# Which engine multiplies attention's probabilities, and which copies the turned ones

## The chip, the cores and the metric

One core of one Trainium2 chip runs the whole layer. The metric is the device time of one execution in microseconds (us); three runs of the kernel before are given. A change of about 0.2% can be told from none.

## The reference

One decoder layer over x of 4096 tokens by 1024 channels, float32. The normed input goes through one projection, whose columns feed three groups of heads of width 64: six heads A (sliding window of 128, two key heads, a learned sink), six heads B (dilated attention, three patterns of 1, 4 and 16 tokens' stride whose results are joined), four heads C (cross-attention to 256 memory tokens). Each result is gated, all go through one output projection, a norm and the residual. The part that the change touches, cut:

```python
p = jnp.exp(s - m[..., None])
denom = jnp.sum(p, axis=-1)
if sink is not None:
    denom = denom + jnp.exp(sink_b - m)
o = jnp.einsum('nbhgqk,nbkhd->nbqhgd', p, vw.astype(jnp.float32))
o = o / jnp.moveaxis(denom, -1, 2)[..., None]
...
wts = jax.nn.softmax(jnp.stack(lses, axis=0), axis=0)
ob = jnp.sum(wts[..., None] * jnp.stack(outs, axis=0), axis=0)
```

## The kernel before, in words

Three stages follow each other: the projection (`project_stage`), attention (`attend_stage`), and the output projection with the norm (`finish_stage`). Before 1053 us the trace is the first stage, after about 1840 us the last.

In attention, `head_group` is built three times, for B, then A, then C. A head is worked in two phases, one for each half of the 4096 queries. A phase has units, each of 128 queries against 256 keys (128 at the sequence's start), and the units go in pairs: 24 pairs a phase for B (12 phases), 8 for A (12 phases) and for C (8 phases), 448 pairs in all. A pair goes through these steps:

- `scores` on TensorE (lines 1353 and 1354): two matmuls a unit into PSUM `ps_s`, which has three places for B and four for A and C; `scores_ready`.
- `scores` on VectorE (line 1455): adds the mask, negates, takes the row maximum while it moves the scores from PSUM to `probs` in SBUF; `max_ready`.
- `scores` on ScalarE (line 1621): the exponential in place, with the row's sum; `sums_ready`.
- Once a phase is through, its coefficients are worked out: for A and C a reciprocal (lines 1471 and 1473), for B an exchange of some dozen small steps (lines 1489 to 1534) that weighs the three patterns; `coef_ready`.
- `scale` (line 1544): VectorE multiplies each unit's probabilities in place by a coefficient for each query; `weighted`.
- `turn` (line 1424): TensorE transposes the pair into PSUM `ps_t`, which has two places; `turned`.
- `copy` (line 1645, or 1648 and 1649 where the two units differ in size): ScalarE copies it to SBUF `pT`, which has four places; `turned_copied`.
- `times_values` (line 1408): TensorE multiplies it with the values, two pairs at a time after each odd pair's next turn; `values_done`. For B the far pattern's banks are kept by ScalarE (line 1658) and added by VectorE (line 1575); the bank is gated by VectorE (lines 1599 and 1609).

The order on each engine is written out by `rounds` and `slots_of`: in a round the new scores of phase a stand beside the turning and multiplying of the phase before, c, and the end of the one before that, b. The slots carry one pair each. Within a slot TensorE does `scores`, `turn`, `exchange`, then `times_values`; VectorE does the `scale` of the pair three slots ahead, `scores`, `copy_queries`, then the read-out of banks; ScalarE does `copy`, `keep`, `scores`, then `copy_queries`. For B the turning of a phase starts 18 slots after its round does, for A and C four; the coefficients come in slot 14 for B and slot 1 for A and C.

`copy_queries` puts B's queries into two further orders, 512 columns at a time: four instructions a phase on ScalarE (line 1674) and four on VectorE (line 1553). A's are shared between the two (lines 1662 and 1555). GpSimd's queue in attention holds seven DMAs that bring parts of the output weights (lines 1921 and 1927), each behind a wait for a finished phase of A or C. All other loads and stores are on SyncE's queue.

In the first stage GpSimd adds weight quarters (lines 943 to 954), casts the first queries (lines 996 and 1004), and VectorE subtracts the rounded part of the weights (line 570) and joins products (lines 621, 644, 739).

Of the kernel before, what the change touches and what calls it, by code (L numbers as in the profile page):

```python
# [27 lines left out]
P = 128  # L28
# [1065 lines left out]
def head_group(nc, io, sc, kind, buf, ctx, prev):  # L1094
# [56 lines left out]
    natural_copied = sem("natural_copied") if kind == "B" else None  # L1151
    k_loaded = [[sem(f"k_loaded{i}{s}") for s in range(2)] for i in range(2)]
    later_keys = buf.early.later_keys
# [5 lines left out]
    scores_ready, max_ready, sums_ready = sem("scores_ready"), sem("max_ready"), sem("sums_ready")  # L1159
    weighted, turned, turned_copied = sem("weighted"), sem("turned"), sem("turned_copied")  # L1160
    values_done = sem("values_done")
    bank_read = sem("bank_read")
    coef_ready = sem("coef_ready")
    step, exps_ready = sem("step"), sem("exps_ready")
    if kind == "B":
# [10 lines left out]
    def number(phase):  # L1176
        return phase[0] * 2 + phase[1]
# [4 lines left out]

    TOTAL = 2 * heads * NP

    def loads(sp):
# [123 lines left out]
    def tensor_parts(pe):  # L1309
# [65 lines left out]
        def times_values(phase, e):  # L1375
# [9 lines left out]
            if kind == "B" and e == 8:  # L1385
                pe.wait_ge(v_loaded[s], 32 * (h + 1))
            pe.wait_ge(turned_copied, p * NP + e + 1)
            bank = bank_of[2 * e]
# [25 lines left out]
        def turn(phase, e):  # L1414
            h, s = phase
            p = number(phase)
            pe.wait_ge(weighted, p * NP + e + 1)
            if prev and isinstance(p, int) and p == 0 and e < 2:
                pe.wait_ge(prev.turned_copied, prev.TOTAL + e - 1)
            ge(pe, turned_copied, p * NP + e - 1)  # L1420
            for j in range(2):
                u = FLAT[s][2 * e + j]
                for at in range(2 - len(u.tiles), 2):
                    last = nc.tensor.transpose(ps_t[:, e % 2, j, at * P:(at + 1) * P],  # L1424
                                               probs[:, s, 2 * e + j, at * P:(at + 1) * P], ident[:])
            last.then_inc(turned, 1)
        return named(scores=scores, exchange=exchange, turn=turn, times_values=times_values)

    def vector_parts(dve):
# [105 lines left out]

        def scale(phase, e):
            h, s = phase
            p = number(phase)
            if e == 0:
                dve.wait_ge(coef_ready, p + 1 + C1)  # L1540
            for j in range(2):
                u = FLAT[s][2 * e + j]
                place = probs[:, s, 2 * e + j, 2 * P - u.keys:]
                last = nc.vector.tensor_scalar(place, place, coef[:, s, u.column:u.column + 1], None, ALU.mult)  # L1544
            last.then_inc(weighted, 1)

        def copy_queries(phase, slot):
            p = number(phase)
            if kind == "B" and slot in N_SLOTS and p > 0:
                if N_SLOTS[slot] == 0:  # L1550
                    dve.wait_ge(q_loaded, 32 * p)
                    dve.wait_ge(scores_ready, p * NP)
                nc.vector.tensor_copy(*natural_piece(N_SLOTS[slot])).then_inc(natural_copied, 1)
            if kind == "A":
                copy_natural(dve, phase, slot, lambda p, g: nc.vector.tensor_copy(
                    *natural_part(p, 2 + g)).then_inc(q_copied, 1))
# [44 lines left out]
        def gated(phase, d):  # L1601
# [7 lines left out]
            nc.vector.tensor_tensor(by, summed.rearrange("p u (r a) -> p u r a", a=32), by, ALU.mult).then_inc(y_ready, 1)  # L1609
        return named(scores=scores, exchange=exchange if kind == "B" else inverse, scale=scale, finish=finish, finish_rest=finish_rest, gated=gated, copy_queries=copy_queries)  # L1610

    def scalar_parts(act):
# [23 lines left out]
        def copy(phase, e):  # L1636
            h, s = phase
            p = number(phase)
            act.wait_ge(turned, p * NP + e + 1)
            if prev and isinstance(p, int) and p == 0 and e < 4:  # L1640
                act.wait_ge(prev.values_done, prev.TOTAL + e - 3)
            ge(act, values_done, p * NP + e - 3)
            a = [2 * P - FLAT[s][2 * e + j].keys for j in range(2)]
            if a[0] == a[1]:
                nc.scalar.activation(pT[:, e % 4, :, a[0]:], ps_t[:, e % 2, :, a[0]:],  # L1645
                                     ACT.Copy).then_inc(turned_copied, 1)
            else:
                nc.scalar.activation(pT[:, e % 4, 0, a[0]:], ps_t[:, e % 2, 0, a[0]:], ACT.Copy)
                nc.scalar.activation(pT[:, e % 4, 1, a[1]:], ps_t[:, e % 2, 1, a[1]:],
                                     ACT.Copy).then_inc(turned_copied, 1)  # L1650

# [8 lines left out]
        def copy_queries(phase, slot):  # L1660
            if kind == "A":
                copy_natural(act, phase, slot, lambda p, g: nc.scalar.activation(
                    *natural_part(p, g), ACT.Copy).then_inc(q_copied, 1))
            p = number(phase)
            if kind != "B" or slot not in Q_SLOTS or isinstance(p, int) and p == 0:
                return
            i = Q_SLOTS[slot]
            if i == 0:
                act.wait_ge(scores_ready, p * NP)
                act.wait_ge(q_loaded, 32 * p)  # L1670
            by = by_residue(q[:, 0, :])
            to = q[:, 1, i * CHUNK:(i + 1) * CHUNK].rearrange("p (b i a) -> p b i a", i=4, a=8)
            of = by[:, 4 * i:4 * i + 4, :].rearrange("p i (b a) -> p b i a", a=8)
            nc.scalar.activation(to, of.bitcast(F32), ACT.Copy).then_inc(q_copied, 1)
        return named(scores=scores, exchange=exchange, copy=copy, keep=keep, copy_queries=copy_queries)

    return named(
        kind=kind, heads=heads, phases=2 * heads, NP=NP, NS=NS, TAIL=TAIL, EARLY=EARLY, TOTAL=TOTAL,
        scores_ready=scores_ready, values_done=values_done, max_ready=max_ready, turned=turned,
        turned_copied=turned_copied, bank_read=bank_read, coef_ready=coef_ready, done_sem=done_sem, y_stored=y_stored,  # L1680
        q_copied=q_copied, copied_by=copied_by, natural_copied=natural_copied,
        loads=loads, tensor_parts=tensor_parts, vector_parts=vector_parts, scalar_parts=scalar_parts)


# [8 lines left out]
def attend_stage(nc, io, sc, early, probs, ahead):  # L1693

    with ExitStack() as ctx:
# [58 lines left out]
        def vector_round(a, c, b):  # L1754
            for i, slot in enumerate(slots_of(a, c, b)):
                if c and c.g.kind != "B":
                    c.parts.exchange(c.phase, i)
                if slot.ahead:
                    x, e = slot.ahead
                    x.parts.scale(x.phase, e)  # L1760
                for v in slot.new:
                    a.parts.scores(a.phase, v)
                if a:
                    a.parts.copy_queries(a.phase, i)
# [12 lines left out]
        def scalar_round(a, c, b):  # L1777
            for i, slot in enumerate(slots_of(a, c, b)):
# [10 lines left out]
                if a:  # L1789
                    a.parts.copy_queries(a.phase, i)  # L1790

        def rounds(eng, round_, parts_of):
# [15 lines left out]
        with nc.Block() as block:  # L1808
# [105 lines left out]
            def _(pool):  # L1914
# [14 lines left out]

                for n in range(4):  # L1930
                    pool.wait_ge(A.done_sem, (9 + n) * NC)
                    load_sum(n)
                for n in range(3):
                    pool.wait_ge(C.done_sem, (1 + n) * NC)
                    load_w(n)
                for g in (B, A):
# [449 lines left out]
```

## Time and profile before

| what | value |
|---|---|
| median of 3 runs | 2163.92 us (2161.46 to 2164.92) |
| span of the profiled execution | 2163.3 us |
| TensorE matmul busy | 2054.7 us (95%) |
| TensorE weight load busy | 1717.7 us (79%) |
| VectorE busy | 1557.3 us (72%) |
| ScalarE busy | 1351.1 us (62%) |
| GpSimd busy | 114.9 us (5%) |
| mean granted TensorE clock | 0.973 |

The execution's own time, outside of its span, isn't given apart from the runs' times above. Busy shares are over the whole span, and the stages differ. PE stands for TensorE's matmuls, PEld for its weight loads, DVE for VectorE, ACT for ScalarE, POOL for GpSimd, SP for SyncE; L1544 is line 1544 of the kernel. A matmul's end is modelled. The granted clock is 1.00 at 2.4 GHz and 0.50 at 1.2 GHz. `a_` stands before the names of attention's own tiles.

### The profile page before, as it was taken

The numbers are of one execution on the slowest core, as the hardware profiler recorded it, in microseconds if no ns is written. First come the engines' busy times: TensorE is split into PE (matmuls) and PEld (weight loads), VectorE is DVE, ScalarE is ACT, GpSimd is POOL, SyncE is SP. The second block draws the span as 40 slices with busy tenths as digits, with TensorE's granted clock in tenths as the row PEclk, the third lists the DMA queues.
The fourth block names the chain that finished last, engine by engine and source line by source line (L and its number), as shares of the span: only waits on it lengthen the run. The fifth ranks groups of instructions, "written<-read, shape, count | busy, mean of one in ns | idle before, by whom it ended". The sixth has DMA issues, their size and how long they took to land. (4 is left out here: it accounts for less than half of the span.)

```text
span 2163.3 us, 39340 instructions
## 1 busy us (share of the span) xinstructions
PE 2054.7 (95%) x12892; PEld 1717.7 (79%) x12892; DVE 1557.3 (72%) x4410; ACT 1351.1 (62%) x3520; POOL 114.9 (5%) x116
## 2 busy tenths in 40 slices
PE   5999899999999999999899999999899998999998
PEld 4787678888888888888777887888778887788886
DVE  6564674546664574446588989989799997888887
ACT  6454454544555464343699979989689998533333
POOL 1232310000000000002000000000000000000000
PEclk7999999999999999999799989989999999999999
DMA  4477576777577657589778676686869996245543
GB/s 157 144 243 217 170 240 179 221 242 218 154 225 223 219 182 244 199 276 273 179 147 157 133 142 135 131 166 121 166 149 214 232 270 179 98 158 175 174 158 113
DMA packets 351737, 401.40 MB, mean 186 GB/s; under 512 B 105617, under 2 KB 255249, under 8 KB 346689
## 3 DMA queue, kind: packets, MB, share of 16 engines
q1 hardware_dynamic: 343120, 364.80, 61.5%
q0 software_dynamic: 8432, 34.30, 5.1%
q8 instruction: 97, 1.59, 0.3%
q14 instruction: 88, 0.71, 0.1%
HBM read 255.62 MB, written 143.39 MB: 184 GB/s over the span
## 5 line engine op out<-in xcount | busy, mean ns | idle before, releaser
L854 PE MATMUL p_ps<-p_u_hi,p_w_hi 128*128 128x512 f32 x1344 | 534.7, 398 | 25.8 <-DVE p_p_c L739 10.6
L856 PE MATMUL p_ps<-p_u_hi,p_w_lo 128*128 128x512 f32 x1344 | 526.8, 392 | 0.0
L855 PE MATMUL p_ps<-p_u_lo,p_w_hi 128*128 128x512 f32 x1344 | 526.2, 392 | 0.0
L570 DVE TENSOR_TENSOR p_w_lo<-p_w_raw,p_w_hi 128x512 fp32r<-128x512 f32 x336 | 245.7, 732 | 331.4 <-ACT p_w_hi L423 329.8
L1621 ACT ACTIVATE probs<-probs,a_stat 128x256 f32<-128x256 f32 (+1 forms) x896 | 433.7, 489 | 49.2 <-DVE a_stat L1455 45.8
L423 ACT ACTIVATE p_w_hi<-p_w_raw 128x512 fp32r<-128x512 f32 x336 | 210.7, 628 | 331.7 <-PE p_ps L856 303.7
L854 PEld LDWEIGHTS p_ps<-p_u_hi,p_w_hi 128*128 128x128 f32 x1344 | 254.1, 189 | 86.1 <-DVE p_u_lo L577 12.0
L856 PEld LDWEIGHTS p_ps<-p_u_hi,p_w_lo 128*128 128x128 f32 x1344 | 254.0, 189 | 54.5
L1455 DVE CUSTOM_DVE_ANT_0 probs<-a_ps_s,fixed 128x256 f32<-128x256 f32 (+1 forms) x704 | 251.6, 396 | 63.2 <-PE a_ps_s L1354 61.9
L855 PEld LDWEIGHTS p_ps<-p_u_lo,p_w_hi 128*128 128x128 f32 x1344 | 254.4, 189 | 50.7
L1408 PE MATMUL a_ps_o<-a_pT,a_v 128*64 128x128 f32 x3320 | 256.7, 285 | 22.8 <-ACT a_pT L1645 21.5
L1424 PE MATMUL a_ps_t<-fixed,probs 128*128 128x128 f32 x1660 | 260.3, 278 | 5.9 <-ACT a_pT L1645 5.1
L1544 DVE TENSOR_SCALAR probs<-probs,a_coef 128x256 f32<-128x256 f32 (+1 forms) x896 | 263.3, 338 | 3.0
L1408 PEld LDWEIGHTS a_ps_o<-a_pT,a_v 128*64 128x64 f32 x3320 | 181.9, 138 | 79.2 <-ACT a_pT L1645 43.8
L1645 ACT ACTIVATE a_pT<-a_ps_t 128x512 f32<-128x512 f32 (+1 forms) x412 | 229.4, 560 | 16.8 <-PE a_ps_t L1424 16.6
L1353 PE MATMUL a_ps_s<-k_hi,q 128*128 128x256 f32 (+1 forms) x672 | 217.3, 342 | 13.0 <-PEq L266 5.9
L1424 PEld LDWEIGHTS a_ps_t<-fixed,probs 128*128 128x128 f32 x1660 | 196.3, 143 | 12.4 <-DVE probs L1544 6.7
L1354 PE MATMUL a_ps_s<-k_lo,q 128*128 128x256 f32 (+1 forms) x672 | 191.7, 302 | 0.0
L1621 ACT ACTIVATION_READ_ACCUMULATOR probs<-probs,a_stat 128x1 f32 x896 | 175.4, 196 | 0.0
L1353 PEld LDWEIGHTS a_ps_s<-k_hi,q 128*128 128x128 f32 x672 | 136.8, 204 | 43.3 <-issue 31.0
L2228 PE MATMUL f_ps<-f_w_lo,parts_hi 128*128 128x512 f32 x384 | 150.4, 392 | 0.0
L2227 PE MATMUL f_ps<-f_w_hi,parts_hi 128*128 128x512 f32 x368 | 144.6, 393 | 5.2 <-DVE probs L2143 4.1
(202 smaller groups left out, 2756.5 us busy)
## 6 DMA issues: line engine op xcount, KB each, us to landing
p_w_raw<-in_w_in SPq DMA_DIRECT2D x156, 256.0 KB, 3.6
p_w_raw<-scratch_w_s SPq DMA_DIRECT2D x144, 256.0 KB, 3.7
scratch_qk_hi<-p_out_a SPq DMA_DIRECT2D x80, 256.0 KB, 4.1
scratch_qk_lo<-p_out_b SPq DMA_DIRECT2D x80, 256.0 KB, 4.2
a_v<-scratch_v SPq DMA_DIRECT2D x40, 512.0 KB, 7.6
scratch_gate<-p_out_a SPq DMA_DIRECT2D x64, 256.0 KB, 3.9
scratch_v<-p_out_a SPq DMA_DIRECT2D x256, 64.0 KB, 2.3
a_gate<-scratch_gate SPq DMA_DIRECT2D x64, 256.0 KB, 5.9
```

Of the source, the lines that this page charges most:

```text
L423: nc.scalar.activation(w_hi[:, m % 3, :, :], w_raw[:, entry(j, g), :, :], ACT.Copy).then_inc(w_hi_ready, 1)
L570: nc.vector.tensor_tensor(w_lo[:, m % 3, :, :], w_raw[:, entry(j, g), :, :], w_hi[:, m % 3, :, :].bitcast(F32), ALU.subtract).then_inc(w_l ...
L854: nc.tensor.matmul(bank, hi, u_hi[j][:, k, :], start=j < 2 and k == 0, stop=False, skip_group_check=True)
L855: nc.tensor.matmul(bank, hi, u_lo[j][:, k, :], start=False, stop=False, skip_group_check=True)
L856: last = nc.tensor.matmul(bank, lo, u_hi[j][:, k, :], start=False, stop=k == KH - 1, skip_group_check=True)
L1353: nc.tensor.matmul(out, w, keys_of(keys_hi, u), start=True, stop=False)
L1408: last = nc.tensor.matmul(place_of(ps_o[j * HD:(j + 1) * HD, bank % 2, :], u), v[name][:, half, tile, :], pT[:, e % 4, j, at * P:(at + 1) ...
L1424: last = nc.tensor.transpose(ps_t[:, e % 2, j, at * P:(at + 1) * P], probs[:, s, 2 * e + j, at * P:(at + 1) * P], ident[:])
L1455: last = nc.vector.tensor_tensor_reduce(out=probs[:, s, 2 * slot + j, a:], in0=ps_s[:, slot % NS, j, a:], in1=masks[u.kind][:, a:], scale= ...
L1544: last = nc.vector.tensor_scalar(place, place, coef[:, s, u.column:u.column + 1], None, ALU.mult)
L1621: last = nc.scalar.activation(place, place, ACT.Exp, scale=-1.0, bias=stat[:, s, 0, u.column:u.column + 1], accum_out=stat[:, s, 1, u.colu ...
L1645: nc.scalar.activation(pT[:, e % 4, :, a[0]:], ps_t[:, e % 2, :, a[0]:], ACT.Copy).then_inc(turned_copied, 1)
```

## The change

The 896 multiplications by coefficients go from VectorE to GpSimd, whose program in attention becomes a round of its own, with its seven DMAs put behind the last multiplication of certain phases. Of the turned pairs, each fourth (number 3, 7, 11, ... in its head group) is copied by VectorE, behind `scores` in its slot; ScalarE copies the others. B's queries that ScalarE put in order are put so by VectorE. The semaphore of the copies becomes two, one for each copying engine, and some semaphores that a head group doesn't use are no longer made. The diff, cut:

```diff
-    weighted, turned, turned_copied = sem("weighted"), sem("turned"), sem("turned_copied")
+    weighted, turned = sem("weighted"), sem("turned")
+    turned_copied = (sem("turned_copied_by_act"), sem("turned_copied_by_dve"))
...
+    def by_dve(n):
+        return n % 4 == 3
+    def wait_copied(eng, n):
+        if n >= 0:
+            eng.wait_ge(turned_copied[by_dve(n)], (n + 1) // 4 if by_dve(n) else n + 1 - (n + 1) // 4)
+    def place_free(eng, p, e):
+        if prev and p == 0 and e < 4:
+            eng.wait_ge(prev.values_done, prev.TOTAL + e - 3)
+        ge(eng, values_done, p * NP + e - 3)
...
-            pe.wait_ge(turned_copied, p * NP + e + 1)
+            wait_copied(pe, p * NP + e)
...
-            ge(pe, turned_copied, p * NP + e - 1)
+            wait_copied(pe, p * NP + e - 2)
...
-        def scale(phase, e):
-            h, s = phase
+        def copy(phase, e):
             p = number(phase)
-            if e == 0:
-                dve.wait_ge(coef_ready, p + 1 + C1)
-            for j in range(2):
-                u = FLAT[s][2 * e + j]
-                place = probs[:, s, 2 * e + j, 2 * P - u.keys:]
-                last = nc.vector.tensor_scalar(place, place, coef[:, s, u.column:u.column + 1], None, ALU.mult)
-            last.then_inc(weighted, 1)
+            if not by_dve(p * NP + e):
+                return
+            dve.wait_ge(turned, p * NP + e + 1)
+            place_free(dve, p, e)
+            a = [2 * P - FLAT[phase[1]][2 * e + j].keys for j in range(2)]
+            if a[0] == a[1]:
+                nc.vector.tensor_copy(pT[:, e % 4, :, a[0]:], ps_t[:, e % 2, :, a[0]:]).then_inc(turned_copied[1], 1)
+            else:
+                nc.vector.tensor_copy(pT[:, e % 4, 0, a[0]:], ps_t[:, e % 2, 0, a[0]:])
+                nc.vector.tensor_copy(pT[:, e % 4, 1, a[1]:], ps_t[:, e % 2, 1, a[1]:]).then_inc(turned_copied[1], 1)
...
         def copy_queries(phase, slot):
+            if kind == "B" and slot in Q_SLOTS and p > 0:
+                i = Q_SLOTS[slot]
+                if i == 0:
+                    dve.wait_ge(scores_ready, p * NP)
+                    dve.wait_ge(q_loaded, 32 * p)
+                nc.vector.tensor_copy(q[:, 1, i * CHUNK:(i + 1) * CHUNK].rearrange("p (b i a) -> p b i a", i=4, a=8),
+                                      by_residue(q[:, 0, :])[:, 4 * i:4 * i + 4, :].rearrange(
+                                          "p i (b a) -> p b i a", a=8).bitcast(F32)).then_inc(q_copied, 1)
...
         def copy(phase, e):
+            if by_dve(p * NP + e):
+                return
...
-            nc.scalar.activation(to, of.bitcast(F32), ACT.Copy).then_inc(q_copied, 1)
...
+    def pool_parts(pool):
+        def scale(phase, e):
+            p, s = number(phase), phase[1]
+            if e == 0:
+                pool.wait_ge(coef_ready, p + 1 + (kind == "A"))
+            for j in range(2):
+                u = FLAT[s][2 * e + j]
+                place = probs[:, s, 2 * e + j, 2 * P - u.keys:]
+                last = nc.gpsimd.tensor_scalar(place, place, coef[:, s, u.column:u.column + 1], None, ALU.mult)
+            last.then_inc(weighted, 1)
...
-                if slot.ahead:
-                    x, e = slot.ahead
-                    x.parts.scale(x.phase, e)
                 for v in slot.new:
                     a.parts.scores(a.phase, v)
+                if slot.pair:
+                    x, e = slot.pair
+                    x.parts.copy(x.phase, e)
...
+        def pool_round(a, c, b):
+            for slot in slots_of(a, c, b):
+                if slot.ahead:
+                    x, e = slot.ahead
+                    x.parts.scale(x.phase, e)
+                    if e == x.g.NP - 1:
+                        x.parts.then_load(x.phase)
...
-                for n in range(4):
-                    pool.wait_ge(A.done_sem, (9 + n) * NC)
-                    load_sum(n)
-                for n in range(3):
-                    pool.wait_ge(C.done_sem, (1 + n) * NC)
-                    load_w(n)
+                def then_load(g):
+                    def load(phase):
+                        n = 2 * phase[0] + phase[1]
+                        if g is A and n >= 8:
+                            pool.wait_ge(A.done_sem, n * NC)
+                            load_sum(n - 8)
+                        if g is C and 2 <= n < 5:
+                            pool.wait_ge(C.done_sem, (n - 1) * NC)
+                            load_w(n - 2)
+                    return load
+                rounds(pool, pool_round, lambda g: named(scale=g.pool_parts(pool).scale, then_load=then_load(g)))
```

## Rows read from the trace of the kernel before

**Rows 1.** Busy time by stretch; columns PE, PEld, DVE, ACT, POOL, clock, DMA share, GB/s
```profile
1088.00:1540.00 452.00, 428.43 (x3992) 368.11 (x3991) 398.33 (x1881) 397.61 (x1381) 0.00 (x0) 0.96 0.73 144
1733.00:1819.00 86.00, 85.91 (x904) 75.82 (x898) 80.03 (x357) 84.36 (x284) 2.81 (x4) 1.00 0.79 216
```

**Rows 2.** Timeline of TensorE's weight loads, 1760 to 1772 us: start, length, instruction
```profile
1760.70 0.19 PEld L1353 LDWEIGHTS a_ps_s<-a_v,q 128*128 128x128 f32 x1 [0.17 <-issue]
...
1761.17 0.46 PEld L1424 LDWEIGHTS a_ps_t<-fixed,probs 128*128 128x128 f32 x4
...
1762.72 0.85 PEld L1408 LDWEIGHTS a_ps_o<-a_pT,a_v 128*64 128x64 f32 x16 [0.17 <-issue]
1763.74 0.19 PEld L1353 LDWEIGHTS a_ps_s<-a_v,q 128*128 128x128 f32 x1 [0.17 <-DVE a_stat L1455]
```

**Rows 3.** Lines 1532 (B's coefficients) and 1473 (C's): duration ns min/median/max, first and last start
```profile
L1532 DVE TENSOR_REDUCE a_coef<-a_picked x12: 209/211/212, 1088.3 to 1539.4; 128x16 f32<-128x64 f32 x12
...
L1473 DVE RECIPROCAL a_coef<-a_stat x8: 253/253/253, 1733.4 to 1818.6; 128x16 f32<-128x16 f32 x8
```

**Rows 4.** Waits, 1088 to 1540 us: us in total, times, longest
```profile
PEld a_ps_o L1408 <- ACT a_pT L1645: 26.7, 55, 1.1
...
PEld a_ps_t L1424 <- DVE probs L1544: 6.0, 8, 1.2
...
PE a_ps_t L1424 <- ACT a_pT L1645: 4.4, 8, 1.0
```

**Rows 5.** Busy time by stretch, 1256 to 1268 us, columns as in rows 1
```profile
1256.00:1262.00 6.00, 4.02 (x35) 2.87 (x33) 5.89 (x28) 4.38 (x16) 0.00 (x0) 1.00 0.27 53
1262.00:1268.00 6.00, 6.00 (x38) 5.22 (x35) 4.35 (x26) 5.71 (x25) 0.00 (x0) 0.57 1.05 221
```

**Rows 6.** Busy time of line 1544 alone: VectorE, clock, DMA share, GB/s
```profile
1088.00:1540.00 452.00, 153.33 (x530) 0.96 0.73 144
```

**Rows 7.** Busy time of the tile pT alone: PE, PEld, ACT, clock, DMA share, GB/s
```profile
1088.00:1540.00 452.00, 147.75 (x1828) 102.39 (x1828) 141.24 (x291) 0.96 0.73 144
```

**Rows 8.** Line 644: duration ns min/median/max
```profile
L644 DVE COPY p_out_b<-p_ps x8: 694/695/696, 235.3 to 998.0; 64x512 f32<-64x512 f32 x8
```

**Rows 9.** Groups by form, 1088 to 1540 us: busy us, mean ns, idle before
```profile
L1645 ACT ACTIVATE a_pT<-a_ps_t 128x512 f32<-128x512 f32 x183 | 107.2, 587 | 4.9 <-PE a_ps_t L1424 4.9
...
L1674 ACT ACTIVATE q<-q 128x512 fp32r<-128x512 f32 x40 | 25.5, 637 | 0.0
...
L1455 DVE CUSTOM_DVE_ANT_0 probs<-a_ps_s,fixed 128x256 f32<-128x256 f32 x394 | 151.6, 420 | 17.6 <-PE a_ps_s L1354 16.9
...
L1553 DVE CAST q<-q 128x512 fp32r<-128x512 f32 x40 | 16.9, 423 | 0.0
```

**Rows 10.** GpSimd's casts by form, and line 943: duration ns min/median/max
```profile
L1004 POOL CAST q<-q 128x2048 fp32r<-128x2048 f32 x1 | 2.4, 2360 | 0.0
L996 POOL CAST q<-q 128x512 fp32r<-128x512 f32 x4 | 2.3, 614 | 3.0 <-DMA q<-scratch_qk_lo 3.0
...
L943 POOL TENSOR_TENSOR p_w_raw<-p_w_raw x12: 1264/1280/1819, 9.0 to 286.5; 128x512 f32<-128x512 f32 x12
```

**Rows 11.** Waits, 1055 to 1088 us
```profile
PEld a_ps_s L1353 <- ACT q L1674: 3.3, 3, 1.7
```

**Rows 12.** Waits, 1540 to 1722 us
```profile
PEld a_ps_o L1408 <- ACT a_pT L1645: 15.2, 27, 1.6
```

**Rows 13.** Timeline of VectorE, 146 to 154 us, and of GpSimd beside it
```profile
146.10 0.69 DVE L570 TENSOR_TENSOR p_w_lo<-p_w_raw,p_w_hi 128x512 fp32r<-128x512 f32 x1 [1.22 <-ACT p_w_hi L423]
...
148.99 0.69 DVE L739 TENSOR_TENSOR p_p_c<-p_ps,p_p_c 128x512 f32<-128x512 f32 x1 [1.06 <-PE p_ps L856]
149.72 1.12 DVE L570 TENSOR_TENSOR p_w_lo<-p_w_raw,p_w_hi 128x512 fp32r<-128x512 f32 x1
...
149.00 1.29 POOL L948 TENSOR_TENSOR p_w_raw<-p_w_raw 128x512 f32<-128x512 f32 x1
150.26 1.74 POOL L949 TENSOR_TENSOR p_w_raw<-p_w_raw 128x512 f32<-128x512 f32 x1
```

More of the change, by code:

```diff
@@ L1151, in head_group @@
     natural_copied = sem("natural_copied") if kind == "B" else None
-    k_loaded = [[sem(f"k_loaded{i}{s}") for s in range(2)] for i in range(2)]
+    k_loaded = [[sem(f"k_loaded{i}{s}") for s in range({"A": 2, "B": 2 - 2 * i, "C": 1 - i}[kind])] for i in range(2)]
     later_keys = buf.early.later_keys
@@ L1163, in head_group @@
     coef_ready = sem("coef_ready")
-    step, exps_ready = sem("step"), sem("exps_ready")
+    step, exps_ready = (sem("step"), sem("exps_ready")) if kind != "C" else (None, None)
     if kind == "B":
@@ L1417, in turn @@
             pe.wait_ge(weighted, p * NP + e + 1)
-            if prev and isinstance(p, int) and p == 0 and e < 2:
-                pe.wait_ge(prev.turned_copied, prev.TOTAL + e - 1)
-            ge(pe, turned_copied, p * NP + e - 1)
+            if prev and p == 0 and e < 2:
+                prev.wait_copied(pe, prev.TOTAL + e - 2)
+            wait_copied(pe, p * NP + e - 2)
             for j in range(2):
@@ L1609, in gated @@
             nc.vector.tensor_tensor(by, summed.rearrange("p u (r a) -> p u r a", a=32), by, ALU.mult).then_inc(y_ready, 1)
-        return named(scores=scores, exchange=exchange if kind == "B" else inverse, scale=scale, finish=finish, finish_rest=finish_rest, gated=gated, copy_queries=copy_queries)
+        return named(scores=scores, exchange=exchange if kind == "B" else inverse, copy=copy, finish=finish, finish_rest=finish_rest, gated=gated, copy_queries=copy_queries)
     def scalar_parts(act):
@@ L1638, in copy @@
             p = number(phase)
+            if by_dve(p * NP + e):
+                return
             act.wait_ge(turned, p * NP + e + 1)
-            if prev and isinstance(p, int) and p == 0 and e < 4:
-                act.wait_ge(prev.values_done, prev.TOTAL + e - 3)
-            ge(act, values_done, p * NP + e - 3)
+            place_free(act, p, e)
             a = [2 * P - FLAT[s][2 * e + j].keys for j in range(2)]
@@ L1645, in copy @@
                 nc.scalar.activation(pT[:, e % 4, :, a[0]:], ps_t[:, e % 2, :, a[0]:],
-                                     ACT.Copy).then_inc(turned_copied, 1)
+                                     ACT.Copy).then_inc(turned_copied[0], 1)
             else:
@@ L1649, in copy @@
                 nc.scalar.activation(pT[:, e % 4, 1, a[1]:], ps_t[:, e % 2, 1, a[1]:],
-                                     ACT.Copy).then_inc(turned_copied, 1)
+                                     ACT.Copy).then_inc(turned_copied[0], 1)
         def keep(phase, d):
@@ L1663, in copy_queries @@
                     *natural_part(p, g), ACT.Copy).then_inc(q_copied, 1))
[L1664 to L1673, printed above, removed]
-            nc.scalar.activation(to, of.bitcast(F32), ACT.Copy).then_inc(q_copied, 1)
-        return named(scores=scores, exchange=exchange, copy=copy, keep=keep, copy_queries=copy_queries)
+        return named(scores=scores, exchange=exchange, copy=copy, keep=keep, copy_queries=copy_queries)
+    def pool_parts(pool):
[8 more added lines that the diff above has]
+            last.then_inc(weighted, 1)
+        return named(scale=scale)
     return named(
@@ L1679, in head_group @@
         scores_ready=scores_ready, values_done=values_done, max_ready=max_ready, turned=turned,
-        turned_copied=turned_copied, bank_read=bank_read, coef_ready=coef_ready, done_sem=done_sem, y_stored=y_stored,
+        wait_copied=wait_copied, bank_read=bank_read, coef_ready=coef_ready, done_sem=done_sem, y_stored=y_stored,
         q_copied=q_copied, copied_by=copied_by, natural_copied=natural_copied,
-        loads=loads, tensor_parts=tensor_parts, vector_parts=vector_parts, scalar_parts=scalar_parts)
+        loads=loads, tensor_parts=tensor_parts, vector_parts=vector_parts, scalar_parts=scalar_parts, pool_parts=pool_parts)
 def load_y(sp, sc, ahead, i, b, rows=(0, KD // 2)):
```

## The prediction, made before the changed kernel ran

> **What bounds the kernel now.** The kernel is three stages in turn: projection (to about 1053 us), attention, output. The change touches attention alone. I read first the busy time by stretches, cut where the head groups change. In the dilated heads' stretch, B, 1088 to 1540 us, TensorE, VectorE and ScalarE are all near full: 428, 398 and 398 of 452 us. In the memory heads' stretch, C, 1733 to 1819, TensorE is at 85.9 of 86; the windowed heads, A, lie between the two [rows 1]. A matmul's end is modelled, so I count where TensorE's weight loads start instead. In C the same place in the program recurs from 1760.70 to 1763.74 us: two pairs in 3.04 us, with only short gaps of 0.17 us where a semaphore had long been given [rows 2]. That is TensorE's own floor: **1.52 us a pair**. The periods of the coefficients stand against it. C has 7 phases from 1733.4 to 1818.6, 12.17 us each or 1.52 a pair: it is at the floor, with ScalarE at 98%. B has 11 phases of 24 pairs from 1088.3 to 1539.4, 41.0 us each or 1.71 a pair [rows 3]. So C can give nothing, and B can give most.
>
> Then the waits. In B TensorE's loads wait 26.7 us (55 times) for ScalarE's copies of turned pairs, 6.0 (8) for multiplied probabilities; its transposes wait 4.4 (8) for those copies too [rows 4]. Every such wait would still leave the 0.17 us gap. What is left is 26.7 - 55 x 0.17 = 17.3, then 4.6 and 3.0: **25 us**. The granted clock is 0.96 over these 452 us [rows 1], so some 36 us ran at its lower level, 1.2 GHz. One such stretch is at hand: from 1256 to 1262 us TensorE was busy 4.02 of 6 us while VectorE was busy 5.89; from 1262 the mean granted clock is 0.57 [rows 5]. Work at half speed costs at most half its length: **18 us**.
>
> **The change, part by part.**
> 1. VectorE loses the multiplications, 153.3 us of B's 452 [rows 6]. It gets a quarter of the copies. These cost ScalarE 141.2 us in B, the read-out of the far banks not among them [rows 7]; a quarter is 35. A VectorE copy of 512 columns out of PSUM took 695 ns [rows 8] against ScalarE's mean of 587 [rows 9], so 42 us on VectorE. It also gets the query casts: 40 in B, at VectorE's 423 ns for a cast of that size 17 us; ScalarE spent 25.5 on them [rows 9]. Sum in B: VectorE 398 - 153 + 42 + 17 = **304 of 452 us**, ScalarE 398 - 35 - 25 = **338**. Both fall clear of TensorE. ScalarE in C ran at 98% and still let TensorE stay at its floor, so I expect no wait from its load.
> 2. GpSimd gets 896 multiplications, 764 of 256 columns and 132 of 128, that is 830 of full width. Nothing in the trace shows its price. Below: its cast, also one input, takes 614 ns at 512 columns and 2360 at 2048, 1.14 ns a column with 0.03 us fixed: 0.32 us. Above: its two-input op takes 1.28 us at 512 [rows 10], 0.64 us at 256 if it goes by size, 1.28 if none of it does. I take 0.45, nearer the cast, whose kind it is, with something for reading the coefficient. A pair then takes 0.9 us against 1.52. It covers itself: the coefficients come three places or more before the first transpose in A and C, four in B. The cover ends at 0.76 us an instruction.
> 3. Copies by VectorE stand behind the maxima of the same place in its queue, two instructions of 0.42 us [rows 9], then 0.69 us of copying, and behind whatever VectorE had in hand before. The pairs it takes are odd ones, which TensorE multiplies last of two: in [rows 2] the transposes begin at 1761.17, the two pairs' values at 1762.72, this pair's half-way through their 0.85 us, so 2.0 us later. Maxima and copy need 0.84 + 0.69 = 1.5, so the copy lands on time if VectorE is free, and late if not. Costed from nothing to its whole 0.69 us, for 112 pairs 0 to 77 us; I take 0.05 each, **6 us** given back, since the DVE has room now. Behind a waiting copy stand the banks' read-out and the next maxima; ps_s has three or four places, which hides it.
> 4. The seven DMAs on GpSimd's queue now stand behind multiplications and wait for a phase finished before the next coefficients come; 0.5 to 0.8 us each, in A's end and C. Nobody needs them until the output stage: nothing. The query cast's wait for its load moves to VectorE one place earlier; the load was asked for long before: nothing. In the first phases ScalarE's query casts held TensorE for 3.3 us [rows 11]; VectorE has room there: 2 us gained.
>
> **Sum.** Waits in B 25, from 1540 to 1722 15.2 - 27 x 0.17 = 11 [rows 12], start 2: 38 us, of which I take 31, as something is always late next (the maxima, then the transposes' places). Of the clock's 18 I take 12, as the fuller TensorE should lose fewer stretches. Less 6 for late copies: 37 us. From the profiled span, 2163.3, that gives 2126; the median is 2163.9, 0.6 above the span, which I let go: **2126 us**. The remaining bound is TensorE.
>
> **Where rule and row meet.** Beside GpSimd's 1.29 us at 149.00, VectorE's 0.69 us op with one input in PSUM and one in SBUF is not lengthened; its op with two inputs in SBUF takes 1.12 us where it took 0.69 at 146.10, with GpSimd idle [rows 13]. So the maxima (PSUM and mask) should run free beside the multiplications, while query casts, gating and small coefficient sums with SBUF inputs may be held. The Trainium skill's page "SBUF — State Buffer" (Who interferes with whom) says this pair of ports is an exclusive lock, held for the whole instruction, and that VectorE's casts and two-input ops take it; the trace agrees for the two-input ops. By that lock all that is held is at most 16 instructions a phase, 12 x 16 x 0.45 = 86 us of VectorE time, on an engine with 100 to spare.
> The page "GPSIMD Engine Reference" (Engine selection) says to keep elementwise work on VectorE, though one-input work goes at about line rate on GpSimd.
>
> **Rivals.**
> (a) The lock or late copies eat the gain. If GpSimd's instruction is 0.64 us and each of 16 a phase waits whole, VectorE gets 12 x 16 x 0.64 = 123 us back, 427 in B, and is as full as before: the time stays at 2155 to 2168. For: the 1.12 against 0.69. Against: mostly an instruction arrives in the middle, or when GpSimd is idle.
> (b) **GpSimd becomes the bound.** Place: TensorE's transposes wait for multiplied pairs. 830 instructions of t must pass between 1088 and 1819, 731 us: it is slower than now from t = 0.88 us. At 1.0 it is 830 - 731 = 99 us more: 2263; at the rows' end of 1.28 some 330 more than now. For: nothing prices the op, and its coefficient has to be fetched. Against: both GpSimd rows scale with size.
> (c) More than forecast: all waits and all the clock, 38 + 18: 2108.
> That the change doesn't do what it says is hard to see: every instruction moves in the program.
>
> **How the numbers follow.** Forecast, 2110 to 2150: 0.66. (c) and beyond: 0.10. (a): 0.10, half of it within 0.2% (4 us, about what a measurement of this kernel tells from no change), a third faster. (b) 0.14, of which a part between 2168 and 2180. Faster 0.80, same 0.05, slower 0.15. The range of 2104 to 2176 leaves out some 0.04 below and 0.12 above.
>
> **What would show it.** GpSimd's multiply of 256 columns at 0.3 to 0.64 us; no or few waits for it by TensorE; B's coefficients every 37.5 to 39 us; C unchanged at 12.2; waits for ScalarE's copies mostly gone, replaced by few for VectorE's; VectorE near 310 of B's time. Wrong if the multiply is over 0.76 us, if TensorE waits for VectorE's copies by tens of us, or if the maxima are longer than 0.42.

## The result, and the profile after

The changed kernel took **2216.5 us** (median of 4 runs, 2211.9 to 2218.8) against 2162.7 us of the kernel before: a ratio of **1.024** (95% interval 1.021 to 1.026), 54 us slower. The forecast was 2126 us, 37 faster. The profiled execution took 2214.3 us with a span of 2212.0; the span before was 2163.3.

First GpSimd, in the groups by form; where [rows 10] had to serve as its nearest relatives, its multiplication now has rows of its own:

```profile
L1702 POOL TENSOR_SCALAR probs<-probs,a_coef 128x256 f32<-128x256 f32 x764 | 705.3, 940 | 0.3
L1702 POOL TENSOR_SCALAR probs<-probs,a_coef 128x128 f32<-128x128 f32 x132 | 80.3, 623 | 57.2 <-DVE a_coef L1548 57.2
```

764 instructions of 256 columns keep it busy for 705 us, on average 0.923 us from start to start; 132 of 128 columns for 80 us, 0.608 each. (The mean length of a single one is a little more, since the next begins before the last has ended.) That is 0.29 us fixed and 2.5 ns a column, where I had taken 0.45 us in all. A little of it is VectorE's doing. Where nothing lengthens them, 18 of 256 columns pass in 16.22 us, 0.900 us each:

```profile
1759.69 16.22 POOL L1702 TENSOR_SCALAR probs<-probs,a_coef 128x256 f32<-128x256 f32 x18
```

Of the 756 distances from one of 256 columns to the next 107 are over 0.915 us, and each of these 107 overlaps a query cast or two-input instruction of VectorE (of the other 649, 284 do); together they add 17 us. By the middle distances, 0.900 and 0.579 us, the fixed part is 0.26 us and a column again 2.5 ns.

Idle time before the multiplications is the one wait until the first coefficients; after that there is none:

Busy time by stretch, columns as in [rows 1]:

```profile
1088.00:1540.00 452.00, 420.78 (x4027) 358.01 (x4026) 329.39 (x1464) 359.44 (x1275) 451.69 (x530) 0.99 0.73 144
1754.00:1858.00 104.00, 90.88 (x895) 75.72 (x894) 59.02 (x260) 79.52 (x269) 103.82 (x117) 1.00 0.63 162
```

GpSimd is at 451.7 of 452 us and 103.8 of 104; VectorE and ScalarE have fallen clear of their 398 us in [rows 1], as forecast, but TensorE is less busy too, 421 us for 428. The waits, 1053 to 1890 us:

```profile
PEld a_ps_t L1440 <- POOL probs L1702: 102.9, 165, 1.4
...
PE a_ps_t L1440 <- POOL probs L1702: 62.7, 141, 1.2
...
PEld a_ps_o L1424 <- ACT a_pT L1672: 11.1, 27, 1.1
PEld a_ps_o L1424 <- DVE a_pT L1561: 6.7, 7, 1.2
```

The waits of [rows 4, 12] for ScalarE's copies, 26.7 and 15.2 us, are down to 11.1; for multiplied probabilities TensorE now waits 103 us at its loads and 63 at its matmuls. Last the coefficients, lines 1548 (B) and 1489 (C), as in [rows 3]:

```profile
L1548 DVE TENSOR_REDUCE a_coef<-a_picked x12: 209/210/213, 1088.0 to 1535.2; 128x16 f32<-128x64 f32 x12
...
L1489 DVE RECIPROCAL a_coef<-a_stat x8: 245/248/253, 1754.7 to 1858.5; 128x16 f32<-128x16 f32 x8
```

Seven periods of C's coefficients take 103.8 us, 14.8 each. That is 16 x 0.923 to within 0.1 us: GpSimd sets the pace. Before it was 12.2, TensorE's floor, so C loses 18.6 us. B's eleven periods take 447.2 us, 40.7 each, where GpSimd's own work is 37.7 us in a phase with short units (27 x 0.923 + 21 x 0.608) and 44.3 in one without, 41.0 in the mean. B had been at 41.0 for other reasons [rows 3], so it is 4 us better and looks untouched. The rest of the loss lies between B's last coefficients and C's first (194.0 us before, 219.5 now: the passage to A, and A) and behind C's last, 9 us. In A and C a pair took less before than 2 x 0.923 us. In the timeline of TensorE's loads in C, beside [rows 2]:

```profile
1766.77 0.19 PEld L1369 LDWEIGHTS a_ps_s<-a_v,q 128*128 128x128 f32 x1 [0.17 <-issue]
...
1768.76 0.42 PEld L1440 LDWEIGHTS a_ps_t<-fixed,probs 128*128 128x128 f32 x4 [0.55 <-POOL probs L1702]
1769.35 0.85 PEld L1424 LDWEIGHTS a_ps_o<-a_pT,a_v 128*64 128x64 f32 x16 [0.17 <-issue]
1770.37 0.19 PEld L1369 LDWEIGHTS a_ps_s<-a_v,q 128*128 128x128 f32 x1 [0.17 <-issue]
```

Two pairs now take 3.60 us, four times GpSimd's 0.900, instead of 3.04, and the transposes' loads sit 0.55 us idle for GpSimd.

### The profile page after: what moved, and what is told of

The parts are those of the page before. It is cut to its first block and busy times, and to the rows that moved or that the text cites. A ratio compares the mean times of both kernels' runs of the same rounds, so it can differ in the third digit from the quotient of the medians.

```text
span 2212.0 us, 39362 instructions
## 1 busy us (share of the span) xinstructions
PE 2059.5 (93%) x12892; PEld 1707.6 (77%) x12892; DVE 1433.0 (65%) x3676; ACT 1296.7 (59%) x3358; POOL 899.6 (41%) x1012
## 5 line engine op out<-in xcount | busy, mean ns | idle before, releaser
L1702 POOL TENSOR_SCALAR probs<-probs,a_coef 128x256 f32<-128x256 f32 (+1 forms) x896 | 784.3, 894 | 57.5 <-DVE a_coef L1548 57.2
L1440 PE MATMUL a_ps_t<-fixed,probs 128*128 128x128 f32 x1660 | 266.3, 280 | 66.8 <-POOL probs L1702 62.7
L1440 PEld LDWEIGHTS a_ps_t<-fixed,probs 128*128 128x128 f32 x1660 | 187.3, 141 | 105.1 <-POOL probs L1702 102.9
L1424 PE MATMUL a_ps_o<-a_pT,a_v 128*64 128x128 f32 x3320 | 240.6, 281 | 10.5 <-ACT a_pT L1672 5.3
L932 POOL DMA_DIRECT2D p_spare<-in_x x24 | 13.2, 551 | 503.2 <-PE p_ps_t L826 425.8
L1672 ACT ACTIVATE a_pT<-a_ps_t 128x512 f32<-128x512 f32 (+1 forms) x306 | 170.8, 558 | 68.6 <-PE a_ps_t L1440 67.5
L1648 ACT ACTIVATION_READ_ACCUMULATOR probs<-probs,a_stat 128x1 f32 x896 | 169.6, 189 | 0.0
```

Source lines behind the costliest of these rows:

```text
L1424: last = nc.tensor.matmul(place_of(ps_o[j * HD:(j + 1) * HD, bank % 2, :], u), v[name][:, half, tile, :], pT[:, e % 4, j, at * P:(at + 1) ...
L1648: last = nc.scalar.activation(place, place, ACT.Exp, scale=-1.0, bias=stat[:, s, 0, u.column:u.column + 1], accum_out=stat[:, s, 1, u.colu ...
L1702: last = nc.gpsimd.tensor_scalar(place, place, coef[:, s, u.column:u.column + 1], None, ALU.mult)
```

## The experiments

Each kernel below is the changed one with one or two edits more. Four of them leave the weighting out in part or whole, and tell of time alone: the one with 128 columns, the one with a constant, and the two with copies. "Before" was run again on each chip beside them; the ratios are to those runs. The theories were GpSimd's rate alone (1), costs in the rest of the change (2), and the order of its queue (3).

**GpSimd multiplies 128 columns of each unit.**

```diff
+                place = probs[:, s, 2 * e + j, P:]
                 last = nc.gpsimd.tensor_scalar(place, place, coef[:, s, u.column:u.column + 1], None, ALU.mult)
```

> The changed kernel, but GpSimd multiplies only the last 128 columns of each unit (the first 128 of a full unit stay unmultiplied). Theory 1, GpSimd's rate alone is the bound: an instruction takes the 0.61 us that the 128-column ones show, 896 x 0.61 = 546 us of work against about 700 us of attention, so the waits for it vanish and the time is what the rest of the change gives: 2120 to 2135 us. Theory 2, the rest of the change costs too (late copies by VectorE, held instructions): the time stays above 2150 although no wait for GpSimd is left. Theory 3, it is the order of GpSimd's queue and not its rate: waits for GpSimd stay over 50 us.

Measured: 2129.7 us (2127.1 to 2132.5), ratio 0.983 (0.979 to 0.987). GpSimd's group by form, the busy time of B, and the waits:

```profile
L1703 POOL TENSOR_SCALAR probs<-probs,a_coef 128x128 f32<-128x128 f32 x896 | 546.2, 629 | 206.8 <-DVE a_coef L1548 146.9 <-DVE a_coef L1487 36.0 <-DVE a_coef L1489 23.8
...
1088.00:1540.00 452.00, 436.22 (x4317) 380.62 (x4317) 340.30 (x1515) 374.94 (x1324) 361.07 (x584) 0.99 0.77 152
...
PEld a_ps_o L1424 <- ACT a_pT L1672: 13.8, 42, 1.2
PEld a_ps_o L1424 <- DVE a_pT L1561: 12.7, 13, 2.2
...
PEld a_ps_t L1440 <- POOL probs L1703: 1.6, 4, 0.7
```

546 us of work, and 1.6 us of TensorE's waits for it. Theory 1 holds. Theory 3 falls, and theory 2 as an account of the loss; a smaller cost of the rest, the late copies, stays. With GpSimd's bound taken away the time is 2130 us where 2126 was forecast. That they are so near is in part luck, since the parts miss in both directions, as shown below. The granted clock of B rises from 0.96 to 0.99.

**A constant in place of the coefficient.**

```diff
-                last = nc.gpsimd.tensor_scalar(place, place, coef[:, s, u.column:u.column + 1], None, ALU.mult)
+                last = nc.gpsimd.tensor_scalar(place, place, 1.0, None, ALU.mult)
```

> The changed kernel, multiplying by the constant 1.0 in place of the coefficient of each query (the weighting is left out), all else the same. If fetching the coefficient is the fixed part of 0.29 us that the two sizes show (0.92 at 256, 0.61 at 128 columns, start to start), an instruction of 256 columns falls to about 0.63 us, 560 us in all, and the time to 2120 to 2140. If the fixed part is the instruction's own, it stays at 0.92 and 2212 us.

Measured: 2149.3 us, one run. Groups by form:

```profile
L1702 POOL TENSOR_SCALAR probs<-probs 128x256 f32<-128x256 f32 x764 | 643.8, 868 | 10.8 <-DVE a_coef L1548 10.6
L1702 POOL TENSOR_SCALAR probs<-probs 128x128 f32<-128x128 f32 x132 | 67.5, 530 | 57.1 <-DVE a_coef L1548 57.1
```

0.843 us start to start at 256 columns, 0.511 at 128. Fetching the coefficient is 0.08 to 0.10 us of each instruction, a third of the fixed part; neither expectation was right. Yet 896 times that is enough to give 67 of the 90 us between the changed kernel and the forecast. GpSimd still has 711 us to do and TensorE's loads still wait 33.4 us for it (80 times), but at 0.84 us an instruction the time is already below the kernel before's.

**A copy in place of the multiplication, and the same one paced.** In the paced kernel GpSimd also waits until the pair four before has been turned.

```diff
                 pool.wait_ge(coef_ready, p + 1 + (kind == "A"))
+            ge(pool, turned, p * NP + e - 3)
...
-                last = nc.gpsimd.tensor_scalar(place, place, coef[:, s, u.column:u.column + 1], None, ALU.mult)
+                last = nc.gpsimd.tensor_copy(place, place)
```

The first, without the added `ge` line:

> The changed kernel, with each multiplication on GpSimd replaced by a copy of the same columns onto themselves (the weighting is left out). If the multiplication is dear because of what it computes, the copy has the price of the first stage's casts, 1.14 ns a column: 0.3 us at 256 columns. If it is dear because of where it runs, beside a busy VectorE on shared ports, the copy is as long, 0.8 to 0.9 us. Time by the first: 2120 to 2135 us; by the second: 2150 to 2212.

Measured: 2169.3 us, one run. GpSimd's group, then the gating instruction (line 1636), duration min/median/max:

```profile
L1702 POOL COPY probs<-probs 128x256 f32<-128x256 f32 x764 | 276.3, 427 | 253.9 <-DVE a_coef L1548 152.2 <-DVE a_coef L1487 54.4 <-DVE a_coef L1489 47.3
...
L1636 DVE TENSOR_TENSOR a_gate<-probs,a_gate x24: 678/692/3852, 1130.1 to 1596.3; 128x512 f32<-128x512 f32 x24
```

The copy takes 0.36 us from start to start, beside the same busy VectorE. So the multiplication is dear for what it computes, not for where it runs, and a cast of the first stage could not tell its price. But the time was not the 2120 to 2135 expected with it. GpSimd, fast now, runs through a phase's 24 pairs without a pause, 48 copies in 17.1 us, and in six of the phases a gating instruction with two inputs in SBUF, 0.69 us before, took 2.9 to 3.85 us. After one of them TensorE was busy for 3.7 us of six (1224 to 1230 us), and its granted clock was 0.72 in the next six. The paced one:

> The run with a copy in place of the multiplication (the weighting is left out), paced in the same way. Unpaced it gave 2169 us although GpSimd was only 41% busy: a gating instruction of VectorE took 3.85 us and the clock fell in six of the stretches. By the theory of unbroken runs the longest gating falls below 1.2 us and the time to 2120 to 2140; if the 2169 us has another cause, it stays over 2155.

Measured: 2129.7 us, one run; the longest gating instruction 0.84 us. B's mean granted clock is 0.98, where it was 0.93 without pacing.

**One two-input instruction for a pair, unpaced and paced.**

```diff
+            u, w = FLAT[s][2 * e:2 * e + 2]
+            if u.keys == w.keys:
+                place = probs[:, s, 2 * e:2 * e + 2, 2 * P - u.keys:]
+                by = coef[:, s, u.column:w.column + 1:w.column - u.column].unsqueeze(2).broadcast_to([P, 2, u.keys])
+                nc.gpsimd.tensor_tensor(place, place, by, ALU.mult).then_inc(weighted, 1)
+                return
```

> The changed kernel, but GpSimd multiplies a pair's two units by one two-input instruction over 512 columns, its second input the two coefficients repeated along the columns. If GpSimd's time is 2.5 ns a column plus a fixed part in each instruction and the two-input form has little of it, as 1.28 us for 512 columns in the first stage says, a pair takes 1.3 us where it now takes 1.84, under TensorE's 1.52: 448 x 1.3 = 580 us, no bound, 2120 to 2140 us. If the repeated operand or VectorE's held ports lengthen it to 1.75 us, as some of those in the first stage, the time is 2190 to 2210.

Measured: 2150.5 us (2145.2 to 2156.9), ratio 0.992 (0.990 to 0.994). The group by form, then the timelines of GpSimd and VectorE from 1106 us:

```profile
L1703 POOL TENSOR_TENSOR probs<-probs,a_coef 128x512 f32<-128x512 f32 x364 | 381.8, 1083 | 154.7 <-DVE a_coef L1548 87.3 <-DVE a_coef L1489 36.2 <-DVE a_coef L1487 27.7
...
1105.97 11.04 POOL L1703 TENSOR_TENSOR probs<-probs,a_coef 128x512 f32<-128x512 f32 x11
...
1106.68 10.61 DVE L1573 CAST q<-q 128x512 fp32r<-128x512 f32 x1
1117.21 0.41 DVE L1505 TENSOR_TENSOR a_moved<-a_stat,fixed 128x256 f32<-128x256 f32 x1
```

A pair costs 1.05 us from start to start (expected: 1.3) where two instructions cost 1.85, and GpSimd is no bound any more: 4.2 us of waits of TensorE's loads for it in B. Yet the time is above the 2120 to 2140 expected. Eleven of its instructions run unbroken from 1105.97 to 1117.01, and a query cast of VectorE that begins at 1106.68, 0.42 us long where nothing holds it, ends at 1117.29, when that run is over. TensorE waits 8.9 us behind it, where the changed kernel waits 3.0 at the same place. The next longest cast of this execution took 1.3 us. The same with the pacing line:

> The run with paired two-input multiplications, and GpSimd starts a pair only when the pair four before it has been turned. In the unpaced run one of VectorE's query casts took 10.61 us, while GpSimd worked through a phase back to back, and TensorE waited 8.9 us behind it. If instructions of VectorE that need the shared ports starve behind an unbroken run of GpSimd's, the pacing leaves gaps of about 0.4 us a pair, the longest cast falls below 1.5 us and the time from 2150 to 2125 to 2140. If each of GpSimd's 1.07 us instructions holds VectorE singly, pacing changes nothing: 2145 to 2155; if GpSimd's later start makes pairs late, more.

Measured: **2138.1 us** (2136.1 to 2145.7), ratio 0.987 (0.985 to 0.989). GpSimd's instructions now come mostly one or two at a time (a few times up to twelve), the longest of B's query casts is 1.2 us (of A's, 1.3), the longest gating instruction 1.5:

```profile
1300.19 2.27 POOL L1704 TENSOR_TENSOR probs<-probs,a_coef 128x512 f32<-128x512 f32 x2 [1.57 <-PE a_ps_t L1440]
1303.24 2.23 POOL L1704 TENSOR_TENSOR probs<-probs,a_coef 128x512 f32<-128x512 f32 x2 [0.78 <-PE a_ps_t L1440]
...
L1580 DVE CAST q<-q x44: 416/418/1215, 1073.7 to 1472.7; 128x512 fp32r<-128x512 f32 x44
...
PEld a_ps_o L1424 <- ACT a_pT L1672: 25.2, 52, 1.7
...
PEld a_ps_o L1424 <- DVE a_pT L1561: 14.2, 19, 1.6
```

This run beats both kernels with the whole computation done.

**Shares of the multiplication for VectorE.** In one kernel VectorE multiplies the first unit of each pair, in one the pairs 1, 5, 9, and so on, in one all of them; each three places ahead, as before. The diff, cut, is that of the last two.

```diff
+        def scale(phase, e):
+            p, s = number(phase), phase[1]
+            if not by_dve_multiplied(p * NP + e):
+                return
...
+            for j in range(2):
+                u = FLAT[s][2 * e + j]
+                place = probs[:, s, 2 * e + j, 2 * P - u.keys:]
+                last = nc.vector.tensor_scalar(place, place, coef[:, s, u.column:u.column + 1], None, ALU.mult)
+            last.then_inc(weighted_dve, 1)
```

> The changed kernel, but of each pair GpSimd multiplies the second unit and VectorE the first, three places ahead as before. GpSimd's work is 393 us and bounds nothing. VectorE gets half of 254 us back: in the dilated heads 304 + 77 = 381 of some 430 us. Theory 1: 2125 to 2140 us, close to the half-columns run. If VectorE's load matters more than I take it, with each multiplication also held by GpSimd's on the shared ports (VectorE's 0.35 us instruction grows toward 0.9), it is the bound and the time 2165 or more.

> The changed kernel, but of the pairs each fourth (1, 5, 9, ..., none of those whose turned pair VectorE copies) is multiplied by VectorE, three places ahead. GpSimd has three quarters of 785 us, 589 of about 700, so it does not bound, and VectorE gets some 64 us back. If VectorE's load is the limit in the run with one unit each, this one with half of that load gives 2135 to 2155 us; if it is that the two engines' multiplications hold each other on each pair, a quarter of the pairs still does it and the time is 2155 to 2170.

> The changed kernel with all multiplications back on VectorE (each fourth copy and the dilated heads' query casts stay there; GpSimd only issues its DMAs). VectorE's busy time in the dilated heads is 398 + 42 + 17 = 457 us against 452 us of that stretch before: it is the bound, and the time is 2180 to 2230 us. If it stays within 2155 to 2175, the copies and casts cost VectorE nothing that matters.

Measured: 2170.9 us (ratio 1.002, 0.999 to 1.005), 2152.0 (0.994, 0.992 to 0.996) and 2198.8 (1.015, 1.012 to 1.018). VectorE's multiplication with one unit each, and the waits; this profiled execution took 2187.6 us, 17 more than the median, so its waits are somewhat above the usual:

```profile
L1559 DVE TENSOR_SCALAR probs<-probs,a_coef 128x256 f32<-128x256 f32 x364 | 141.6, 392 | 2.4
...
L1559 DVE TENSOR_SCALAR probs<-probs,a_coef 128x128 f32<-128x128 f32 x84 | 31.1, 374 | 0.7
...
PEld a_ps_o L1424 <- DVE a_pT L1570: 33.2, 35, 5.0
...
PEld a_ps_o L1424 <- ACT a_pT L1681: 16.5, 49, 1.5
```

Before, the means were 348 and 282 ns; now 392 and 374. With each fourth pair they are 489 and 404. So the two multiplications do hold each other, by 0.04 to 0.14 us in the mean, much less than a whole instruction of GpSimd. TensorE waits 33.2 us for VectorE's copies, which come late as soon as VectorE is loaded: here, and 33.3 us in B alone with all multiplications on VectorE, whose busy time there is 424 of 452 us. The steps from all of them to half and a quarter, 2199, 2171, 2152, go with VectorE's busy time in B, 424, 386 and 375 us. That its load alone makes them isn't shown, since the holding and the clock differ as well: B's granted clock was 0.95, 0.91 and 0.94 in these three profiled executions, and 0.99 with 128 columns. The multiplication had to leave VectorE before it could take copies and casts; the last of the three shows what these cost alone, some 33 us.

**All turned pairs copied by ScalarE.** Once on the changed kernel, once on the paired and paced one.

```diff
-        return n % 4 == 3
+        return False
...
-            eng.wait_ge(turned_copied[by_dve(n)], (n + 1) // 4 if by_dve(n) else n + 1 - (n + 1) // 4)
+            eng.wait_ge(turned_copied[0], n + 1)
```

> The changed kernel with all turned pairs copied by ScalarE again (the query casts stay on VectorE). If GpSimd's rate alone is the bound, this changes nothing: 2205 to 2220 us. If late copies by VectorE add to it, it is faster by 10 us or more; if ScalarE's relief was worth something, slower.

Measured: 2223.0 us (2222.0 to 2226.7), ratio 1.028 (1.026 to 1.030). With GpSimd the bound this should have changed nothing, and it is 6 us more. GpSimd's work is 713.4 + 81.9 = 795 us here instead of 785. The middle distance at 256 columns is 0.900 us in both kernels. What grew is the time that VectorE holds it up: 117 distances over 0.915 us, each beside a cast or an instruction with two inputs, add 25 us, where 107 added 17; those beside gating instructions are 17 instead of 8. So the bound's own length depends on where VectorE's instructions fall. Why they fall worse here is open.

> The paired and paced run, with all turned pairs copied by ScalarE (the query casts stay on VectorE). There TensorE still waits 14.2 us for VectorE's copies and 25.2 for ScalarE's. If the quarter of the copies on VectorE is worth its late arrivals, ScalarE is full again (some 370 + 36 of 452 us in the dilated heads) and TensorE's waits for it grow: 2145 to 2160 us. If the late copies of VectorE cost as much as ScalarE's relief gives, it stays at 2138, within 5 us; below 2133 the copies should never have moved.

Measured: **2130.5 us** (2128.1 to 2133.8), ratio 0.983 (0.980 to 0.985), the fastest kernel of the study that does the whole computation. Busy time of B, and the waits:

```profile
1088.00:1540.00 452.00, 436.16 (x4238) 380.78 (x4238) 338.05 (x1428) 401.48 (x1394) 295.14 (x313) 0.98 0.77 152
...
PEld a_ps_o L1424 <- ACT a_pT L1672: 29.9, 94, 0.8
```

ScalarE is at 401 of 452 us, as full as before, and TensorE's waits for it are 29.9 us but short, 94 of them with none over 0.8 us; 53 are the gap of 0.17 us alone. Without that gap 14 us are left. The same kernel with a quarter of the copies on VectorE waited 25.2 for ScalarE and 14.2 for VectorE, 71 times, of which 27 us are left. So moving copies to VectorE seems to cost more than it brings once VectorE is rid of the multiplications. No run of one kernel is within the range of the other's (2128.1 to 2133.8 against 2136.1 to 2145.7), but the two ratios' intervals meet at 0.985, so the difference of 8 us is likely and not certain.

## Why the prediction was wrong

- **The step that failed is the price in part 2, "I take 0.45".** The multiplication takes 0.92 us. I bounded it by 0.32 and 1.28 us and chose by kinship, "nearer the cast, whose kind it is". Kinship of inputs was the wrong measure: a copy of the same columns costs 0.36 us, a multiplication 0.92, with a constant 0.84. It is 2.5 ns a column and 0.29 us fixed in each instruction. The casts of [rows 10] have less of both, 1.14 ns and 0.03 us, and the two-input row has one size only, so it could tell nothing of a fixed part (the paired form shows 0.574 us at 256 columns and 1.002 at 512 where nothing lengthens it, 0.15 us fixed and 1.7 ns a column). The upper end, 1.28, held the value; the choice between the ends was made without a reason from size or price.
- **"The cover ends at 0.76 us an instruction"** fits the runs: at 0.61 us TensorE's loads wait 1.6 us for GpSimd, at 0.84 they wait 33.4. Rival (b) was right as a mechanism: its place (TensorE's transposes wait for GpSimd) and its sum. It counted 830 full-width instructions, which at 0.923 are 766 us, 35 more than its 731. A short unit costs two thirds of a full one and not half, so the work is 785 us, 54 more: what was measured by the medians (49 between the two profiled spans). Its 0.14 was too little for a case whose decisive price the text itself called unknown, with the crossing, 0.88, in the middle of the bounds.
- **The range** left out 12% above 2176 us. Between 0.32 and 1.28 us more than a third lies over 0.92. The range was made from the chosen value and not from the bounds.
- Part 1 was right in direction and low in size: VectorE was to have 304 us in B and ScalarE 338; with 128 columns they are 340 and 375, in a stretch that holds 8% more work (4317 matmuls for 3992), so 315 and 347 for the same work. Both are clear of TensorE all the same. B's coefficients come every 38.0 us, within the 37.5 to 39 forecast, but C, which was to stay at 12.2 us a phase, takes 12.7 (1690.9 to 1779.9 us). The 2130 us against 2126 is thus a sum in which the misses cancel in part, and with the bound taken away.
- Part 3, late copies, was right in kind and low in size: 12.7 us of waits for them with 128 columns, 14.2 paired and paced, against 6 allowed. Part 4 was right that nobody waits for GpSimd's DMAs; the 2 us at the start did not come in the changed kernel, where B's first coefficients are at 1088.0 us (1088.3 before).
- Of "where rule and row meet", the maxima indeed run free, 0.42 us in all kernels. Rival (a), the lock, did not eat the gain in the changed kernel: B's query casts took up to 0.67 us and A's up to 0.94, and their means were 0.47 to 0.53. There it was also VectorE that held GpSimd, by 17 us in all. VectorE was held far longer in kernels that I had not thought of, where GpSimd is faster: up to 10.6 us for one cast. What the Trainium skill's page "GPSIMD Engine Reference" (Engine selection) says of one-input work, that it goes at about line rate on GpSimd, is not what this multiplication shows, at 2.5 ns a column; the copy's 0.36 us is nearer to it. The same page's advice to keep elementwise work on VectorE was borne out for the change as made, and not for the paired and paced form.

## What to carry to other kernels

Before elementwise work is moved to an idle engine, its instruction must be priced there by operation and by size: number of instructions times the fixed part, plus columns times the slope, against the time that the present bound takes for the same work. If the crossing lies inside the bounds of that price, the forecast has two signs, and one run with half the columns tells which. Joining two small instructions in one can save more than the move is worth (here 1.85 to 1.05 us a pair on GpSimd). Where two engines hold each other, as GpSimd and VectorE did here, look in the trace for long unbroken runs of the one and for single long instructions of the other, and try giving the work in portions.

## What the runs showed of the hardware

- GpSimd, from start to start, in the mean and, in brackets, in the middle one, which nothing lengthens: multiplication by a coefficient for each partition 0.923 us at 256 columns (0.900) and 0.608 at 128 (0.579); with a constant 0.843 (0.816) and 0.511 (0.495); the copy 0.36 (0.344) at 256; the two-input form with the second input repeated along the columns 1.05 (1.002) at 512.
- An instruction of VectorE with two inputs in SBUF, or a cast from SBUF to SBUF, can be held for many of GpSimd's instructions, not only for one: a cast 10.6 us behind eleven two-input ones, to the end of their run, and a gating instruction up to 3.85 us within a run of 48 copies, which went on for 2.3 us after it. In 785 us of back-to-back multiplications by a coefficient the longest cast was 0.94 us. What lets VectorE in between these and not between those was not tried; that the fixed part leaves a gap is a guess.
- The holding goes both ways. Of GpSimd's multiplications in the changed kernel 107 came late by 17 us in all, each beside a cast or a two-input instruction of VectorE, while VectorE's maxima, with one input in PSUM and one in SBUF, stayed at 0.42 us in every kernel.
- With a wait of four pairs' distance on GpSimd's queue both long holds were gone, and the times fell: 2150.5 to 2138.1 us, and, for the copies, 2169.3 to 2129.7, one run of either.
